# An S5 layer whose second half of input products is computed early and kept in SBUF

## The reference

```python
def body(h, u_blk):
    bu = jnp.einsum('blgc,gpc->blgp', u_blk.astype(jnp.complex64), b_bar)
    bu = bu.at[:, 0].add(lam_bar * h)
    a = jnp.broadcast_to(lam_bar, bu.shape)
    _, hs = lax.associative_scan(_linear_combine, (a, bu), axis=1)
    y = jnp.real(jnp.einsum('blgp,gcp->blgc', hs, c_c)) + d_g * u_blk
    return hs[:, -1], y
...
ag = jax.nn.gelu(y).astype(x.dtype) @ w['w_glu'][o]
mix = ag[..., :D_MODEL] * jax.nn.sigmoid(ag[..., D_MODEL:])
```

## Time and profile before

| | |
|---|---|
| median of three runs | 1042.61 us |
| the profiled execution | 1042.72 us, span 1040.9 us |
| TensorE matmul busy | 939.4 us (90%) |
| TensorE weight load busy | 577.3 us (55%) |
| VectorE busy | 470.0 us (45%) |
| GpSimd busy | 318.1 us (31%) |
| ScalarE busy | 196.8 us (19%) |
| mean granted TensorE clock | 0.971 of full |
| moved by DMA | 292.14 MB, 281 GB/s on average |

### The profile page before, as it was taken

The page is one execution under the profiler, slowest core; times in us unless marked ns, Lnnn a source line. Parts: engine busy times, 40 slices in busy tenths (PEclk is TensorE's granted clock), DMA queues, the critical chain, the costliest instruction groups (busy, mean ns, idle before and its releaser), DMA issues.

```text
span 1040.9 us, 15791 instructions
## 1 busy us (share of the span) xinstructions
PE 939.4 (90%) x5788; PEld 577.3 (55%) x5788; DVE 470.0 (45%) x1014; ACT 196.8 (19%) x386; POOL 318.1 (31%) x554
## 2 busy tenths in 40 slices
PE   4999989999999888878889599999999999777786
PEld 4888878645565444444445585444556555434352
DVE  4500254686652265776537861122565333121227
ACT  5422132322310000000045331004331000000003
POOL 1278920095222146666402720000021111101100
PEclk9999999999899998988999899999999999999999
DMA  7128770847679999999982937540077999999965
GB/s 256 41 82 289 290 309 1 329 169 305 233 280 420 398 422 422 411 399 374 349 336 63 167 110 316 249 162 21 20 290 305 427 419 427 423 423 425 421 245 201
DMA packets 45930, 292.14 MB, mean 281 GB/s; under 512 B 10737, under 2 KB 12017, under 8 KB 26391
## 3 DMA queue, kind: packets, MB, share of 16 engines
q1 hardware_dynamic: 35463, 269.92, 66.1%
q0 software_dynamic: 8640, 16.03, 4.1%
q10 hardware_dynamic: 1760, 5.31, 1.7%
HBM read 270.10 MB, written 36.80 MB: 295 GB/s over the span
## 4 chain that ended last, share of the span: by engine, by line
PE 63%; DMA 18%; DVE 10%; SPq 4%; issue 2%; ACT 1%; DVEq 0%; POOL 0%; POOLq 0%; ACTq 0%
PE ps L824 14%; PE ps L1144 10%; PE ps L967 9%; DMA arena<-in_w_down 8%; PE ps L1123 7%; DMA arena<-in_w_gu 6%; PE ps L1387 5%; DVE arena L2205 4%; DVE arena L1794 3%; PE ps L1041 2%; SPq L601 2%; PE ps L1071 2%; SPq L597 2%; PE ps L786 2%; PE ps L997 1%
## 5 line engine op out<-in xcount | busy, mean ns | idle before, releaser
L1144 PE MATMUL ps<-arena 128*64 128x256 f32 x2048 | 232.8, 384 | 29.6 <-DMA arena<-in_w_gu 29.6
L1144 PEld LDWEIGHTS ps<-arena 128*64 128x64 f32 x2048 | 148.5, 138 | 117.3 <-DMA arena<-in_w_gu 31.8
L2477 POOL TENSOR_TENSOR arena<-arena 128x32 f32<-128x32 f32 (+5 forms) x233 | 117.4, 504 | 165.7 <-DMA arena<-in_s_d 70.0
L824 PE MATMUL ps<-arena 128*128 128x256 f32 (+1 forms) x640 | 142.1, 383 | 0.3 <-ACT arena L1499 0.3
L1123 PE MATMUL ps<-arena 128*64 128x512 f32 x512 | 124.7, 631 | 12.2 <-DMA arena<-in_w_down 11.3
L824 PEld LDWEIGHTS ps<-arena 128*128 128x128 f32 x640 | 121.0, 190 | 19.1 <-ACT arena L1499 0.5
L967 PE MATMUL ps<-arena 128*128 128x512 f32 x256 | 114.5, 597 | 0.8 <-DMA arena<-in_w_out 0.7
L1644 ACT ACTIVATE arena<-ps 128x128 f32<-128x128 f32 x64 | 17.7, 277 | 441.0 <-PE ps L1144 441.0
L2216 DVE TENSOR_TENSOR arena<-arena,ps 128x128 f32<-128x128 f32 x64 | 17.9, 287 | 172.2 <-ACT arena L1644 170.3
L1123 PEld LDWEIGHTS ps<-arena 128*64 128x64 f32 x512 | 37.4, 145 | 78.4 <-issue 71.7
L967 PEld LDWEIGHTS ps<-arena 128*128 128x128 f32 x256 | 47.0, 190 | 54.9 <-issue 52.9
(11 more groups left out here) (232 smaller groups left out, 1022.3 us busy)
## 6 DMA issues: line engine op xcount, KB each, us to landing
arena<-in_w_gu SPq DMA_DIRECT2D x64, 2048.0 KB, 14.3
arena<-in_w_down SPq DMA_DIRECT2D x64, 1024.0 KB, 13.2
arena<-in_w_in SPq DMA_DIRECT2D x10, 1024.0 KB, 6.5
scratch_yd<-arena SPq DMA_DIRECT2D x2, 4160.0 KB, 17.4
arena<-scratch_yd SPq DMA_DIRECT2D x16, 512.0 KB, 7.4
arena<-in_w_out SPq DMA_DIRECT2D x1, 4096.0 KB, 12.2
scratch_hd<-arena ACTq DMA_DIRECT2D x8, 512.0 KB
arena<-in_w_glu SPq DMA_DIRECT2D x2, 2048.0 KB, 8.0
```

The costliest lines, as they stand in the source:

```text
L824: mm = pe.matmul(o[:, b, 0:WIDTHS[b]], w[:, kc, (n % 2) * P:(n % 2 + 1) * P], tokens_of_half(kc, b), start=kc == 0, stop=kc == KC - 1)
L1144: mm = pe.matmul(ps[CAP * f:CAP * f + CAP, 2 + s, 0:256], XT[l][:, kc, CAP * s:CAP * s + CAP], w[:, kc, 256 * f:256 * f + 256], start=kc = ...
L2477: step(g_.tensor_tensor(out, a, b, op))
```

## The change

1. VectorE rotates all eight batches in a row; the first scan comes behind the eighth. It waits for the second half's tables ahead of the fifth.
2. The input products of batches 4 to 7 become PSUM jobs of their own (`yi` 4 to 7), listed ahead of `y` 0. ScalarE copies each of them to SBUF (`YI`). `from_states` of these batches then stands alone in its `y` job, and VectorE, which emptied it by a copy, adds `YI` while it empties.
3. Accordingly the taps of half 1 are wanted first: SyncE's queue issues all eight of half 1, then the second half's tables, then all eight of half 0. ScalarE issues none.
4. `YI` takes the place that `TT[1]` had; `TT[1]` and `WGL_HALVES[1]` are in the spare buffer (`SPARE_AT`). `WGL_HALVES[1]` is loaded once `yi` 7 is full, `WGL_HALVES[0]` and `WGL` as before.
5. Of layer 1's first expert weights, expert 3's is loaded once `y` 7 was emptied, expert 6's (it goes into the spare buffer) after the GLU.
6. GpSimd's `first_states` stands behind all eight `add_turned`.

```diff
--- before.py
+++ after.py
@@ -162,7 +162,7 @@
     for q in range(1, 4):
         j += [(("u", q + 1), "act"), (("zs", q), "dve")]
     j += [(("u", q), "act") for q in (5, 6, 7)] + [(("zs", q), "dve") for q in (4, 5, 6)]
-    j += [(("zs", 7), "dve")] + [(("y", q), "act") for q in range(4)] + [(("yT", 0), "act"), (("yT", 1), "act")]
+    j += [(("zs", 7), "dve")] + [(("yi", q), "act") for q in range(4, 8)] + [(("y", q), "act") for q in range(4)] + [(("yT", 0), "act"), (("yT", 1), "act")]
     for q in range(4, 8):
         j += [(("y", q), "dve"), (("yT", q - 2), "act")]
     j += [(("yT", q), "act") for q in (6, 7)]
@@ -388,9 +388,10 @@
         SHT = place(scratch_at, PAIRS, NS)
         SKIP = place(A + 21504, KC, CW)
         HEND = place(A + 23296, 2, PAIRS)
-        TT = [place(at, 2 * 4, L * KQ) for at in (A + 14336, A + 28832)]
+        TT = [place(at, 2 * 4, L * KQ) for at in (A + 14336, SPARE_AT)]
+        YI = place(A + 28832, 4, D, parts=SC)
         YT = place(A + 18432, KC, NT)
-        WGL_HALVES = [place(at, KC // 2, D) for at in (A + 14336, A + 28832)]
+        WGL_HALVES = [place(at, KC // 2, D) for at in (A + 14336, SPARE_AT)]
         WGL = place(A + 32928, KC, D)
         SIG = [place(A + 5120 + 512 * b, 512) for b in range(2)]
         GT = [place(A + 6144 + 512 * b, 512) for b in range(2)]
@@ -401,6 +402,10 @@
             out = YK[q // 4][0:SC, :, (q % 4) * P:(q % 4 + 1) * P]
             return (out.rearrange("p l (j b c) -> p b j l c", b=2, c=CW)[:, b],
                     slot("y", q)[0:SC, b, :].rearrange("p (j l c) -> p j l c", j=4, l=L))
+
+        def inputs_view(q, b):
+
+            return YI[:, q - 4, 512 * b:512 * b + 512].rearrange("p (j l c) -> p j l c", j=4, l=L)
 
         hd, yd, kp = T["hd"], (T["yd0"], T["yd1"]), T["kp"]
         sdk, sdq, sdd = T["sdk"], T["sdq"], T["sdd"]
@@ -726,16 +731,15 @@
             sp.dma_start(kv[:, :, KZERO:KROW // 2], KS.rearrange("p n l w -> p n (l w)")).then_inc(sem("taps_out"), 16)
             sp.wait_ge(sem("taps_out"), 16)
             sp.wait_ge(sem("h_2"), 5)
-            for s in range(L // 2):
-                taps(sp, s, 0)
+            for s in range(L):
+                taps(sp, s, 1)
             ring.wait_full(sp, "zs", 1)
             sp.wait_ge(sem("turns_in"), 16)
             load_turns(1)
-            for s in range(L // 2, L):
+            for s in range(L):
                 taps(sp, s, 0)
-            ring.wait_full(sp, "zs", 7)
-            for s in range(L // 2):
-                taps(sp, s, 1)
+            ring.wait_full(sp, "yi", 7)
+            load(WGL_HALVES[1], T["w_glu"][0][:, 4:8], "w_in_1")
             sp.wait_ge(sem("ends_ready"), 4)
             sp.dma_start(T["s5_p"], HEND).then_inc(sem("stored"), 16)
             sp.dma_start(T["s5_sr"], SHR).then_inc(sem("stored"), 16)
@@ -743,17 +747,17 @@
             ring.wait_full(sp, "y", 3)
             load(WGL_HALVES[0], T["w_glu"][0][:, 0:4], "w_in_0")
             ring.wait_full(sp, "y", 7)
-            load(WGL_HALVES[1], T["w_glu"][0][:, 4:8], "w_in_1")
             load(WGL, T["w_glu"][1], "w_out_in")
             ring.wait_full(sp, "yT", KC - 1)
             load_first(1, 0, 0)
             load_gate_up(1, 1, 0, 1)
             for b in range(2):
                 load_down(1, 0, 0, b)
+            ring.wait_emptied(sp, "y", 7)
+            load_gate_up(1, 3, 1, 1)
+            ring.wait_full(sp, "gl", 0, TILES)
+            load_gate_up(1, 2, 1, 0)
             load_first(1, 6, 1)
-            ring.wait_full(sp, "gl", 0, TILES)
-            for s in range(2):
-                load_gate_up(1, 2 + s, 1, s)
             sp.wait_ge(sem("routed"), routed(1, "main", 4))
             for s in range(2):
                 load_gate_up(1, 4 + s, 2, s)
@@ -1303,19 +1307,20 @@
                                            start=True, stop=True)
                 full(mm)
 
-            def outs_of(pr):
-                return [slot("y", pr // 4)[0:SC, b, pr % 4 * P:(pr % 4 + 1) * P] for b in range(2)]
-
-            def from_inputs(pr, start=True):
-                for b, out in enumerate(outs_of(pr)):
-                    pe.matmul(out, U[:, 2 * pr + b, NS:UC], taps_of_group(pr, b), start=start, stop=False,
-                              skip_group_check=True)
-
-            def from_states(pr):
+            def outs_of(name, pr):
+                return [slot(name, pr // 4)[0:SC, b, pr % 4 * P:(pr % 4 + 1) * P] for b in range(2)]
+
+            def from_inputs(name, pr, start, stop):
+                for b, out in enumerate(outs_of(name, pr)):
+                    mm = pe.matmul(out, U[:, 2 * pr + b, NS:UC], taps_of_group(pr, b), start=start, stop=stop,
+                                   skip_group_check=True)
+                return mm
+
+            def from_states(pr, alone):
                 for h_, g_ in ((HR, GR), (HI, GI)):
-                    for b, out in enumerate(outs_of(pr)):
+                    for b, out in enumerate(outs_of("y", pr)):
                         half = slice(64 * b, 64 * b + 64)
-                        mm = pe.matmul(out, h_[half, pr], g_[half, pr, 1:L + 1], start=False, stop=h_ is HI,
+                        mm = pe.matmul(out, h_[half, pr], g_[half, pr, 1:L + 1], start=alone and h_ is HR, stop=h_ is HI,
                                        skip_group_check=True)
                 return mm
 
@@ -1343,26 +1348,30 @@
             for q in (4, 5, 6):
                 driven(q)
             driven(7)
+            pe.wait_ge(sem("taps_in_1"), 16 * L)
+            for q in range(4, 8):
+                ring.wait_free(pe, "yi", q)
+                for j in range(4):
+                    mm = from_inputs("yi", 4 * q + j, True, True)
+                full(mm)
             pe.wait_ge(sem("taps_in_0"), 16 * L)
             ring.wait_emptied(pe, "us")
             for q in range(4):
                 ring.wait_free(pe, "y", q)
                 for j in range(4):
-                    from_inputs(4 * q + j, start=j == 0)
+                    from_inputs("y", 4 * q + j, j == 0, False)
             for q in range(4):
                 wait_states(q)
                 for j in range(4):
-                    mm = from_states(4 * q + j)
+                    mm = from_states(4 * q + j, False)
                 full(mm)
             turned(0)
             turned(1)
-            pe.wait_ge(sem("taps_in_1"), 16 * L)
             for q in range(4, 8):
                 ring.wait_free(pe, "y", q)
                 wait_states(q)
                 for j in range(4):
-                    from_inputs(4 * q + j)
-                    mm = from_states(4 * q + j)
+                    mm = from_states(4 * q + j, True)
                 full(mm)
                 turned(q - 2)
             turned(6)
@@ -1731,10 +1740,11 @@
             for q in range(3, 8):
                 u_out(q)
             decays(1)
-            act.wait_ge(sem("taps_out"), 16)
-            ring.wait_full(act, "zs", 7)
-            for s in range(L // 2, L):
-                taps(act, s, 1)
+
+            for q in range(4, 8):
+                take(act, "yi", q)
+                src = slot("yi", q)[0:SC]
+                give(act, a.copy(YI[:, q - 4].rearrange("p (b n) -> p b n", b=2), src), "yi", q)
 
             def y_out(q):
                 take(act, "y", q)
@@ -2398,12 +2408,11 @@
                 tt(hr[:, :, 1:NCH], hr[:, :, 1:NCH], y[:, :, 0:n], ALU.subtract)
                 tt(hi[:, :, 1:NCH], hi[:, :, 1:NCH], x[:, :, 0:n], ALU.add)
 
-            for q in range(4):
+            for q in range(8):
+                if q == 4:
+                    dve.wait_ge(sem("turns_in"), 32)
                 rotated(q)
             scanned(0)
-            dve.wait_ge(sem("turns_in"), 32)
-            for q in range(4, 8):
-                rotated(q)
             ring.wait_full(dve, "u", 7)
             states(0, 0, PAIRS // 2)
             dve.sem_inc(sem("states_in"), 1)
@@ -2415,8 +2424,12 @@
             dve.wait_ge(sem("ends_ready"), 3)
             for q in range(4, 8):
                 take(dve, "y", q)
-                step(v.tensor_copy(*y_views(q, 0)))
-                give(dve, v.tensor_copy(*y_views(q, 1)), "y", q)
+                for b in range(2):
+                    out, states_part = y_views(q, b)
+                    ins = v.tensor_tensor(out, states_part, inputs_view(q, b), ALU.add)
+                    if b == 0:
+                        step(ins)
+                give(dve, ins, "y", q)
 
             def gated(ch, k):
                 i = ORDER[k] if ch else k
@@ -2735,11 +2748,9 @@
             ring.wait_emptied(pool, "k", 1)
             tt(KS[:, :, 0], KS[:, :, 0], SKIP.rearrange("p (n q) c -> p n (q c)", n=2), ALU.add)
             pool.sem_inc(sem("s5_parts"), 1)
-            for q in range(4):
+            for q in range(8):
                 add_turned(q)
             first_states()
-            for q in range(4, 8):
-                add_turned(q)
             last_states(0)
```

## The result

The changed kernel takes 1045.12 us (median of 20 runs, 1039.64 to 1047.68) against 1041.72 for the kernel before (20 runs, 1031.44 to 1047.68): ratio 1.0034 [1.0018, 1.0051], so about 3.5 us slower. The forecast was 1046.1, 3.5 us above the three runs known then.

What follows compares the result with a forecast made beforehand. Before 609.61 VectorE sets the pace in S5, then TensorE; the DMA engines are full from 570 to 600 us. 1040.9 span + 1.8 around it + 3.5 = 1046.2, hence 1046.1; range 1041 to 1050.

Steps and rivals of the forecast that it cites:

- The tables: SyncE's queue in S5: four more taps in front, 2.1 us each, land the second half's tables 8.4 us later, at 592.4.
- slower still: Rival, chance 0.13: taps writing 16 partitions keep to 107 GB/s, 2.45 us each; the kernel takes 1048 to 1051 us.
- the rate belongs to half 1: Rival, chance 0.08: 202 GB/s comes from half 1's taps, not from two queues; some 5.5 us less, 1037 us.
- much faster: Rival, chance 0.03: all transfers land in time, the GLU starts at 622.0, 9.6 us less; 1033 us.
- no difference: Rival, chance 0.16: eight taps in one row go at 160 GB/s or so, 1.6 us each; 1044.0 us.
- Half 0's last tap: SyncE's queue: half 0's taps come last, first at 593.0, eighth at 607.7, where all were there at 591.8 before.
- VectorE's chain: Rotations, scans and states run behind the late tables; VectorE takes up batch 4's output at 627.8, 13.0 us later.
- Which path is last: GLU start: VectorE's path 635.0, TensorE's 633.3 to 635.6 (634.5 in the middle); taken as 635.1, 3.5 us later.
- The covers: Weight loads, expert 3 and 6's exchange and ScalarE's four copies were to hide; emptying with addition too was costed at 0.
- Passing through: Behind the GLU the experts are bound by their loads, so the 3.5 us delay reaches the kernel's end whole.

Runs made afterwards that it cites:

- e1: The changed kernel with each half's eight taps replaced by one DMA over all 128 partitions (content not right); ratio 0.9912 to the kernel before.
- e2: The changed kernel with half of the taps on ScalarE's queue: SyncE writes partitions 0 to 63, ScalarE 64 to 127; ratio 0.9977 to the kernel before.
- e5: The changed kernel with taps lacking their leading zeros (GpSimd writes them), tables behind four taps of half 1; 1031.33 us, ratio 0.9916 to the kernel before.
- e4: The changed kernel with the second half's tables issued behind four taps of half 1 instead of eight; ratio 1.0037 to the kernel before.
- e7: The changed kernel with the first half's scan moved back behind the fourth rotation; ratio 1.0017 to the kernel before.
- e8: The kernel before with taps lacking their leading zeros (GpSimd writes them), half 1's taps in the spare buffer; ratio 0.9985 to the kernel before.
- e3: The changed kernel with half of the taps on ScalarE's queue, both queues writing on both sides of partition 64; ratio 0.9992 to the kernel before.
- e6: The changed kernel with seven unused matmuls on TensorE ahead of its wait for half 0's taps; ratio 1.0029 to the kernel before.

## Why the prediction was right, step by step

- **The tables.** Forecast: there at 592.4, which is +22.5 (from 569.92). Measured: +21.7. The rate was 131 to 133 GB/s and not 125. Over stretches of 8 us one queue showed neither 107 nor 202, so "slower still", "the rate belongs to half 1" and "much faster" are out. So is "no difference", which wanted 160.
- **Half 0's last tap.** Forecast 607.7, +37.8; TensorE took its products up at +37.8. Eight taps behind the tables took 16.1 us (600.77 less 584.66) against 15.3 (607.7 less 592.4), and the tables were 0.8 us earlier than forecast: the two misses cancel. The one in the taps is the first of them, which landed 1.9 us behind the tables (565.63 plus 20.9, less 584.6) where I had 0.6.
- **VectorE's chain.** Forecast: through with its states and ready for batch 4 at 627.8, +57.9; measured +56.5. From the take-up of batch 4's rotation to the GLU I had 42.5 us (635.0 less 592.5), and where this path binds it takes 42.6 (e1, e2, e5). The first pair of scans and the states of half 0 are 12.8 us together in either order: 4.63 + 8.13 before, 5.27 + 7.50 after.
- **Which path is last: the step that was mis-sized.** I had VectorE's path at 635.0 (+65.1) and TensorE's at 634.5 (+64.6) in the middle of 633.3 to 635.6, from 25.6 to 27.9 us behind the taps. TensorE took 28.3 (629.09 less 600.77): the products stood at the slow end (8.87, clock 0.79), and a second-half batch with its transposes takes 2.55 us (617.87 to 620.43) where I had 2.4. VectorE's path had 1.9 us to spare: 584.66 plus 42.6 is 627.2, and its rows show it waiting 0.53 and 1.15 us. e4 and e7, in which it is freed by 7.5 and 4 us, show that it doesn't bind. So the path that I took for the last (by 0.5 us) was 0.9 too late, and the one that is last came 1.5 later than its middle. That the sum came out so near (+66.1 for +65.2) is in part luck: the two paths lie close together.
- **The covers.** The four `yi` copies are 1.01 us each and are over before 600.77. An emptying with addition takes 1.41 us for two, as a pair of copies took before. `WGL_HALVES[0]`, issued at 617.44, landed 9.0 us later at 626.4, 2.6 us ahead of the GLU (forecast 2). These cost nothing, as put. The new order of the loads for experts 3 and 6 stands in every kernel above but before and e8, and no run took it back alone; that it costs nothing is only known as far as the last point goes.
- **Passing through.** The last two columns of the table agree within the intervals, but for e7's, whose +5.0 is just above the end of its own (+4.7): what the GLU's place wins or loses comes out at the end, as far as intervals of 2 to 5 us to either side can tell. The experts load at 421 GB/s with a share of 1.01, as in the earlier trace rows.

The rival "much faster" had sized what the order is worth when all transfers are in time: the GLU at 622.0, +52.1, 9.6 us less. e1 and e5 show +52.8 and +52.3. What the prediction didn't ask is what it would take to have that. The order needs the taps sooner than the one before, and its queue gives them later; with taps in time it is worth 9 us, with these it costs 3.5.

## What to carry to other kernels

Before work is pulled ahead, price what it reads: ask how many bytes stand in front of the last input in its queue, and at what rate that kind of transfer runs, which the GB/s of its own stretch tells and the DMA share does not. When two paths come out within a microsecond, say that either may bind, and size both from the slow end. Bytes that are known constants, zeros here, are cheaper written on the chip than fetched: the same reordering went from 3.5 us lost to 9 us won.

## What the hardware showed beyond that

- One DMA over 128 partitions ran at 394 GB/s; eight over 16 each, with the same bytes and the same 2 KB pieces, at 125 to 133. Two queues with such narrow DMAs made 202 when they wrote 64 partitions apart and 151 when 32.
- TensorE stood still just before the last batch of L1305 with no releaser that the profile shows, and longer the more tap traffic there was: 0.37 us in e1, e5 and e8 (there a release by ScalarE), 1.48 before, 2.5 in e4, 2.8 in e2, 3.4 in e3, 4.8 in e6, 5.0 in after and e7. A packet of one of the profile's `instruction` queues lies some 3 to 4 us ahead of the restart in before, after and e7 (at 579.5, 575.5 and 582.5). That TensorE waits there for instructions that are loaded through the same DMA engines is a guess; no run took that apart. It lies where the tables are awaited anyway.
